# Hybrid attention layer: rope 1 ahead of the last unit's gate on VectorE, and branch A's division moved to ScalarE

## The reference, cut to what matters

```python
# branch A, per block of 128 queries, keys of this and the last block
s = einsum(q, k) * dh ** -0.5                 # masked to distances 0..127
m = maximum(max(s), sink)
p = exp(s - m)
denom = sum(p) + exp(sink - m)
o = einsum(p, v) / denom
y_a = (o * silu(gate_a)) @ w_pa
```

## Time and profile before

| | before |
|---|---|
| median of 3 runs | 1384.58 us (1383.91 to 1384.93) |
| the profiled execution | 1384.04 us |
| its span, first to last instruction | 1382.2 us |
| PE busy | 1357.1 us, 98% |
| ACT busy | 591.9 us, 43% |
| DVE busy | 487.8 us, 35% |
| POOL busy | 670.6 us, 49% |
| granted TensorE clock, mean | 0.997 |

### The profile page before, as it was taken

The page is one execution under the profiler, slowest core; times in us unless marked ns, Lnnn a source line. Parts: engine busy times, 40 slices in busy tenths (PEclk is TensorE's granted clock), DMA queues, the critical chain, the costliest instruction groups (busy, mean ns, idle before and its releaser), DMA issues.

```text
span 1382.2 us, 19897 instructions
## 1 busy us (share of the span) xinstructions
PE 1357.1 (98%) x6432; PEld 1146.7 (83%) x6432; DVE 487.8 (35%) x878; ACT 591.9 (43%) x1035; POOL 670.6 (49%) x512
## 2 busy tenths in 40 slices
PE   9999999899999999999999999999999999999996
PEld 7877878788988988898898888888888888888885
DVE  5876665772031222203011011010101202297688
ACT  5465565553462365347237322222222222345442
POOL 4633443454555555446454465464555646422214
PEclk9999999999999999999999999999999999999998
DMA  8442232336374355337434343654536445377674
GB/s 256 132 128 77 76 126 56 122 107 137 93 162 128 100 108 152 118 96 163 148 110 138 88 149 114 150 129 101 182 91 152 116 142 140 103 236 260 207 245 163
DMA packets 204992, 190.08 MB, mean 138 GB/s; under 512 B 16529, under 2 KB 178577, under 8 KB 204945
## 3 DMA queue, kind: packets, MB, share of 16 engines
q1 hardware_dynamic: 191344, 151.74, 37.2%
q0 software_dynamic: 13600, 37.75, 11.1%
HBM read 185.23 MB, written 41.94 MB: 164 GB/s over the span
## 4 chain that ended last, share of the span: by engine, by line
PE 68%; issue 16%; POOL 11%; DMA 2%; DVE 1%; ACT 1%; POOLq 0%; SPq 0%; ACTq 0%
PE acc L1540 61%; POOL w_lo L577 6%; POOL w_lo L576 5%; PE ps_scores L1540 2%; DMA raw<-w_in 1%; PE ps_out L1540 1%; PE ps_turn L1540 1%; PE ps_out L1630 1%; PE ps_turn L1602 0%; DMA raw<-w_out 0%; DVE z L1398 0%; PE ps_scores L1567 0%; DMA raw<-xT 0%; PE ps_scores L1564 0%; DVE x_lo L999 0%
## 5 line engine op out<-in xcount | busy, mean ns | idle before, releaser
L576 POOL TENSOR_TENSOR w_lo<-raw,w_hi 128x512 fp32r<-128x512 f32 x242 | 323.1, 1335 | 695.0 <-ACT w_hi L630 572.0
L1540 PE MATMUL acc<-x_hi,w_hi 128*128 128x512 f32 x1216 | 478.9, 394 | 4.4 <-DVE q_a L1024 2.9
L1540 PE MATMUL acc<-x_hi,w_lo 128*128 128x512 f32 x1216 | 474.2, 390 | 0.0
L1540 PE MATMUL acc<-x_lo,w_hi 128*128 128x512 f32 x1216 | 474.0, 390 | 0.0
L630 ACT ACTIVATE w_hi<-raw 128x1024 fp32r<-128x1024 f32 x224 | 234.4, 1057 | 335.7 <-PE acc L1540 328.2
L577 POOL TENSOR_TENSOR w_lo<-raw,w_hi 128x512 fp32r<-128x512 f32 x242 | 332.5, 1374 | 0.0
L1540 PEld LDWEIGHTS acc<-x_hi,w_hi 128*128 128x128 f32 x1216 | 228.5, 188 | 51.6 <-DVE q_a L1024 4.2
L1540 PEld LDWEIGHTS acc<-x_hi,w_lo 128*128 128x128 f32 x1216 | 228.2, 188 | 48.1
L1540 PEld LDWEIGHTS acc<-x_lo,w_hi 128*128 128x128 f32 x1216 | 228.5, 188 | 43.9
L1263 DVE TENSOR_TENSOR part_a<-acc,part_a 128x512 f32<-128x512 f32 x16 | 11.1, 691 | 321.7 <-PE acc L1540 321.5
L1540 PE MATMUL acc<-w_hi,x_lo 128*128 128x384 f32 x256 | 85.6, 334 | 0.0
(11 more groups left out here) (275 smaller groups left out, 1610.9 us busy)
## 6 DMA issues: line engine op xcount, KB each, us to landing
raw<-w_in SPq DMA_DIRECT2D x384, 128.0 KB, 2.2
q_left<-w_out POOLq DMA_DIRECT2D x12, 2048.0 KB, 13.4
raw<-w_in SPq DMA_DIRECT2D x256, 96.0 KB, 2.5
raw<-q_left SPq DMA_DIRECT2D x32, 512.0 KB, 4.7
raw<-w_in SPq DMA_DIRECT2D x64, 192.0 KB, 2.9
raw<-w_pa SPq DMA_DIRECT2D x64, 128.0 KB, 5.9
raw<-w_out SPq DMA_DIRECT2D x16, 512.0 KB, 4.3
raw<-xT SPq DMA_DIRECT2D x8, 512.0 KB, 4.8
```

Of the source, the lines that this page charges most:

```text
L576: nc.gpsimd.tensor_tensor(dst[:, left], raw[:, slot, left], hi[:, left].bitcast(F32), ALU.subtract)
L1540: ins = nc.tensor.matmul(into[:, 0:cols], s, m, start=start and k == 0, stop=stop and k == n - 1)
```

## The change

Three edits. First, ACT scales branch A's probabilities (`divide_a`), at the place where DVE did, after a wait for the reciprocal, which stays on DVE. Second, at an iteration's end `rope_q(i, 1)` comes ahead of unit 7's `gate_out` on DVE; `gate_out` moves from place 26 to 28. Third, the split of the second gate tile is taken out of `gate_out` (`split_last`) and in branch A's iterations stands behind the gate of bank 2, at place 29. In branch B's first iteration it still follows `gate_out` directly.

```diff
+            def divide_a(u, a):
+                act.wait_ge(recip_ready, a + 1)
+                for hh in range(2):
+                    p = probs_a[:, u % 2, hh, (P if u % 4 == 0 else 0):2 * P]
+                    last = nc.scalar.activation(p, p, ACT.Copy, scale=rdenom[:, u % 2, hh:hh + 1])
+                last.then_inc(normalised, 1)
...
+                    if stage == "normalise":
+                        divide_a(u, first_unit + u)
                     if stage == "collect":
...
                 nc.vector.reciprocal(rdenom[:, j, 0:2], denom[:, j, 0:2]).then_inc(recip_ready, 1)
-                dve.wait_ge(recip_ready, a + 1)
-                for hh in range(2):
-                    p = probs_a[:, j, hh, (P if u % 4 == 0 else 0):2 * P]
-                    last = nc.vector.tensor_scalar(p, p, rdenom[:, j, hh:hh + 1], None, ALU.mult)
-                last.then_inc(normalised, 1)
...
                 nc.vector.tensor_tensor(g, across[:, u % 2, :], g, ALU.mult).then_inc(gated_a, 1)
-                if b == 3 and j == 1:
-                    dve.wait_ge(gated_a, a + 1)
-                    split_gated(kind, gate_a[:, j, :], i + A_ITERS * j, i * 2 + j)
+
+            def split_last(i):
+                dve.wait_ge(gated_a, unit_a(i) + A_UNITS)
+                split_gated("a", gate_a[:, 1, :], i + A_ITERS, i * 2 + 1)
...
-                    if with_attention and ("values", A_UNITS - 1) in A_PLAN.get(g, ()):
-                        gate_out("a", A_UNITS - 1, unit_a(i - 1) + (A_UNITS - 1), i - 1)
                     if A_BLOCKS[g - 1][2:4] == (A_JOBS - 1, 1):
                         rope_q(i, 1)
+                        if with_attention:
+                            gate_out("a", A_UNITS - 1, unit_a(i - 1) + (A_UNITS - 1), i - 1)
                     if last and bank >= 2:
                         gate(by_block(gate_a[:, bank - 2, :]), by_residue(acc[bank][:]), bank, i * 2 + (bank - 2))
+                    if with_attention and last and bank == 2:
+                        split_last(i - 1)
...
                         gate_out("a", A_UNITS - 1, unit_a(A_ITERS - 1) + (A_UNITS - 1), A_ITERS - 1)
+                        split_last(A_ITERS - 1)
```

## The result

| | before | changed |
|---|---|---|
| median | 1384.43 us (1383.91 to 1384.93, 4 runs) | 1396.4 us (1395.9 to 1397.22, 4 runs) |
| the profiled execution, its span | 1384.04, 1382.2 | 1397.22, 1395.4 |
| ratio to before | | 1.0087, 95% interval 1.0070 to 1.0105 |

The sign and the mechanisms were as forecast. The size was not: +6.35 us were worked out, with 8.6 as the upper bound, and the median moved by 12.0.

A forecast was written before the change was run, and what follows sets the result against it. PE, busy 98% of the span, was taken as the bound, with 6.8 us of waits to remove. Pass 1 +0.25, passes 2 and 3 +1.4 each, pass 4 +3.3 gave +6.35: median 1390.9 us, range 1382.5 to 1393.5.

The forecast's parts named there:

- The pass end: Before passes 2, 3 and 4: rope 1's wait goes, but the uncovered sigmoid makes mask 0 0.6 late, ScalarE's queue 1.0.
- The head of passes 2 and 3: Units 0 to 2: turn at 201.4, not 200.43; second values step +1.25; unit 2 gives back 0.25.
- The failed step: Passes 2 and 3 from unit 3: chain 5.0 to 5.4 us against 5.5, a cast costs 0.1 to 0.8; +1.4 per pass.
- Pass 4's casts: Pass 4: a cast between exponential and division in every unit, two at unit 6; +3.3 us, between 1.6 and 4.2.
- The bounds: Summed over the passes: +3.3 to +8.6 us around +6.35; median 1387.9 to 1393.2 for the slower case.
- Rival A: Passes: VectorE, freed of the division, delivers low half and mask earlier; faster, 1376.5 to 1381.5, around 1380 us; chance 0.16.
- Rival C: Division free, each of three pass ends costs 1.0 to 1.1: 1387.8 us; chance inside the slower case's 0.66.
- Rival B: Mask 0 in time, pass ends keep 1.2 us each, cancelling the division's cost in passes 1 and 4: 1384.6; chance 0.18.

The follow-up runs named there:

- order_only: Changed kernel with the division back on VectorE, so only the new pass-end order against the kernel before: 1387.45 against 1384.72 us, +2.7.
- split_first: Changed kernel with the split directly behind unit 7's gate, ahead of bank 2's gate: 1395.41 us, +11.0 against the kernel before.
- divide_late_gate: Kernel before with the division on ScalarE and each unit's sum and gate behind the next low half and mask: 1385.31 against 1384.72 us, +0.6.
- idle_pair: Kernel before, VectorE dividing, plus a pair of unused Copies on ScalarE at the division's place: 1393.05 against 1384.28 us, +8.8.
- late_gate_split: `before_late_gate` with the split two places later, behind VectorE's division: 1382.14 us against 1384.37 for the kernel before, -2.2.
- before_late_gate: Kernel before, division on VectorE, with each unit's sum and gate one place later: 1390.81 against 1384.28 us, +6.5.

## Why the prediction had the sign right and the size wrong

- **The pass end held.** Sigmoid (199.16 - 3.66 = 195.50, forecast 195.5), mask and the scores of unit 1 came within 0.1 us of the walk. Alone it cost 0.87 to 0.89 us each (`order_only`, +2.7 in all), and about half of that is the sigmoid's lost cover (`split_first`, 0.45 each).
- **The head of passes 2 and 3 was sized a little too high.** At unit 0 the turn is 0.6 us late within the old frame (204.70 - 3.66 = 201.04, against 200.43 and a forecast of 201.4), at unit 1 0.95 (forecast 1.25), at unit 2 0.67 (1.0). The half-width division pair takes 0.68 us, not 0.8, and VectorE, freed of its own, gave unit 2 of pass 1 0.6 back.
- **The failed step** is the one that begins "From unit 3 on, the chain turn, `probs_out`, low half, mask, exponential, division is 5.0 to 5.4 us against 5.5". That chain leaves out the branch that joins it on VectorE: division, moves of halves, sum, gate, low half. The prediction named `move_halves` as queued behind the new wait and then gave it no price. With the division of 0.9 ahead of it, this branch is the longer one in the units behind a cast, and POOL stretches its gate multiply from 0.29 to 0.95. Measured from unit 2 to 7: 1.6 us in each of passes 1 to 3 and 4.5 in pass 4, against 0.4 and 1.9. With the branch out of the way (`divide_late_gate`) each of passes 1 to 3 loses 0.45, which is what the single chain gave. `idle_pair` (+8.8) shows that this branch alone can make nearly the whole loss, and `divide_late_gate` (+0.6) that most of it goes with the branch. The direct way is no free ride: set against `late_gate_split`, which has the late gate too, the division on ScalarE still costs 2.8 us. The two prices don't add up, since a unit is late by the longer of its two ways.
- **Pass 4's casts** were named as the cause of its 3.3 us, and in part they are: with the late gate, unit 6 still loses 1.06 us behind two casts, where the walk had 1.25. That pass 4 as a whole then loses only 0.4 is because the late gate gains 1.09 at unit 3. In units 3 to 5, where the walk had 0.25 and the changed kernel lost 1.36, the branch is the difference: without it (`divide_late_gate` against `late_gate_split`) the division costs 0.2 there. The prediction puts a cast between exponentials and division in every unit; at unit 7 there is none, but a copy out of `acc` of 1.2 us.
- **The bounds** failed with the step: its term was set to 0.1 to 0.8 for a pass by the slack of a single chain. Of the 5.65 us between +6.35 and +12.0, passes 1 to 3 hold some 2.8 (1.14 + 2 x 2.37 measured, against 0.25 + 2 x 1.4), pass 4 2.5 (5.78 against 3.3).
- **Rival A** (relief by the port rule) had a real part: no division takes longer than 0.91 us any more, and unit 2 of pass 1 gained 0.6 us. But the wait at the values of unit 0 of pass 4 didn't go; it only changed its cause, from VectorE's low half to the high half that ScalarE copies late (the first line is from before):

```profile
261.61 0.39 PE L1618 MATMUL ps_out<-probsT_lo,v_pair 128*128 128x256 f32 x1 [1.19 <-DVE probsT_lo L1099]
267.71 0.38 PE L1626 MATMUL ps_out<-probsT_hi,v_pair 128*128 128x256 f32 x1 [1.18 <-ACT probsT_hi L711]
```

  Its sign wasn't met either: in the third pass `probs_out(0)` starts at 206.68 - 3.66 = 203.02, not before 201.9. Rival C had the price of its part nearly right (1387.8, measured 1387.45), and its other half, a free division, wrong. Rival B needed a mask in time, and it wasn't.

## What to carry to other kernels

When work is moved to another engine, write out for every unit what is queued behind it there, follow each of those to the engine that waits for it, and look at what that engine has queued behind in turn; a chain with slack of its own says nothing if a branch joins it. A result that nobody needs soon (here the sum and gate) shouldn't stand in an in-order queue ahead of one that is needed at once. And a wait that is taken away at one place should be followed to the next thing that the same engine must deliver: here rope 1 came early and the mask came late.

## What the runs showed of the hardware

- A pair of 128x256 VectorE scalings that takes 0.62 us alone took 2.53 when it started 0.17 us behind POOL's subtraction; each of the two (1.27 and 1.35) ended some 0.15 behind one of POOL's two instructions (`before_late_gate`). With the split behind it, it starts 0.80 us ahead of POOL (108.04 and 108.84 in `late_gate_split`) and takes 0.62 again, worth 1.8 us each time.
- A VectorE multiply with both inputs in SBUF, 128x128, takes 0.29 us alone. In the changed kernel's passes it took 0.70 to 1.00 at 11 places where it started under a POOL subtraction, and ended 0.14 to 0.16 behind that. Where it fell on the seam of two POOL instructions, it took 0.29 (before, 104.76): a shift of some tenths can turn the one into the other.
- PE's turns are so regular that a profile resolves 0.05 us: in `order_only` the lateness stays at 0.32 for seven turns, which medians with a spread of 3 us can't show.
